# A 16-unit attention layer: six units' probabilities turned by 32x32 squares through DRAM, two table copies moved, bias windows kept as raw runs

## The reference

```python
def _na_mixer(h, hc, w_in, rpb, w_out, need_ctx_out):
    q, k, v, g = jnp.split(h @ w_in, 4, axis=-1)          # 16 heads of 64
    kc, vc = jnp.split(hc @ w_in[:, WIDTH:3 * WIDTH], 2, axis=-1)
    ...
    s_loc = s_loc + bias[None]                            # rpb by relative place, inside a window
    s_ctx = jnp.einsum('brqhd,bchd->bhrqc', q, kc)
    logits = jnp.concatenate([s_loc, s_ctx], axis=-1)
    p = jax.nn.softmax(logits, axis=-1)
    o = p_loc @ v + p_ctx @ vc                            # written here as products
    y = (o * jax.nn.silu(g)) @ w_out
```

## Time and profile before

| | us |
|---|---|
| median of 3 runs | 1814.83 (1814.77 to 1815.89) |
| the profiled execution, its own time | 1815.61 |
| its span in the profile | 1813.8 |
| PE busy in the span | 1793.3 |
| DVE, ACT, POOL busy | 954.2, 901.5, 1366.0 |
| the attention loop, first scores to the last turned unit | 303.9 to about 375.5 of the span |

### The profile page before, as it was taken

One profiled execution on the slowest core, in us unless ns is written; L12 is line 12 of the kernel. 1 busy time (PEld: TensorE's weight loads), 2 busy tenths in 40 slices (PEclk: granted clock), 3 DMA queues, 4 the chain that ended last, 5 costly groups with the idle time before them and its releaser, 6 DMA issues.

```text
span 1813.8 us, 24988 instructions
## 1 busy us (share of the span) xinstructions
PE 1793.3 (99%) x9274; PEld 1477.5 (81%) x9274; DVE 954.2 (53%) x1756; ACT 901.5 (50%) x1329; POOL 1366.0 (75%) x568
## 2 busy tenths in 40 slices
PE   6999999999999999999999999999999999999999
PEld 5888888887889888887788888888888878888887
DVE  4673766778755524866653230713095876143152
ACT  3324424674455644456554644464445565555452
POOL 2624544559968898977689798969897867888885
PEclk9999999999999999999999999999999999999999
DMA  9863885749775775565665566567655666656663
GB/s 366 291 210 94 270 310 163 198 141 312 244 277 200 211 221 191 180 198 168 209 186 192 179 195 191 193 187 234 191 193 185 192 190 182 196 160 210 190 195 128
DMA packets 206457, 372.91 MB, mean 206 GB/s; under 512 B 33508, under 2 KB 59092, under 8 KB 205780
## 3 DMA queue, kind: packets, MB, share of 16 engines
q1 hardware_dynamic: 203328, 363.69, 63.5%
q10 hardware_dynamic: 3028, 7.86, 1.2%
HBM read 367.27 MB, written 9.28 MB: 208 GB/s over the span
## 4 chain that ended last, share of the span: by engine, by line
PE 97%; DVE 2%; DMA 0%; issue 0%; ACTq 0%; ACT 0%; POOL 0%; DVEq 0%
PE ps L1300 26%; PE ps L1302 25%; PE ps L1301 25%; PE ps L1426 3%; PE ps L1427 3%; PE ps L1428 3%; PE ps L1992 1%; PE ps L1993 1%; PE ps L1994 1%; PE ps L1348 1%; PE ps L1697 1%; PE ps L1918 1%; PE ps L1668 1%; PE ps L1678 1%; PE ps L1962 1%; PE ps L1558 1%
## 5 line engine op out<-in xcount | busy, mean ns | idle before, releaser
L659 POOL TENSOR_TENSOR w_lo<-raw,w_hi 128x1024 fp32r<-128x1024 f32 x556 | 1347.1, 2461 | 397.4 <-ACT w_hi L697 376.2
L1300 PE MATMUL ps<-w_hi,act_rows_r 128*128 128x512 f32 x2064 | 814.8, 395 | 3.2 <-POOL w_lo L659 3.1
L1302 PE MATMUL ps<-w_hi,act_rows_r 128*128 128x512 f32 x2064 | 805.2, 390 | 0.0
L1301 PE MATMUL ps<-w_lo,act_rows_r 128*128 128x512 f32 x2064 | 804.6, 390 | 0.0
L697 ACT ACTIVATE w_hi<-raw 128x1024 fp32r<-128x1024 f32 x556 | 571.1, 1058 | 371.0 <-DMA raw<-in_ffn_w_up 100.8
L1300 PEld LDWEIGHTS ps<-w_hi,act_rows_r 128*128 128x128 f32 x2064 | 388.2, 188 | 90.4 <-issue 9.1
L1302 PEld LDWEIGHTS ps<-w_hi,act_rows_r 128*128 128x128 f32 x2064 | 388.0, 188 | 82.0
L1301 PEld LDWEIGHTS ps<-w_lo,act_rows_r 128*128 128x128 f32 x2064 | 388.4, 188 | 77.7
L2647 DVE STREAM_TRANSPOSE ps<-proj 32x256 f32<-32x256 f32 (+1 forms) x384 | 166.5, 434 | 6.5
L2628 DVE TENSOR_TENSOR proj<-proj,ps 128x1024 f32<-128x1024 f32 (+1 forms) x18 | 20.4, 1132 | 252.2 <-PE ps L1302 247.9
L1426 PE MATMUL ps<-act_rows_r,w_hi 128*128 128x512 f32 (+1 forms) x288 | 101.3, 352 | 0.0
(11 more groups left out here) (245 smaller groups left out, 1554.0 us busy)
## 6 DMA issues: line engine op xcount, KB each, us to landing
raw<-in_w_in SPq DMA_DIRECT2D x120, 512.0 KB, 3.9
raw<-in_ffn_w_gate SPq DMA_DIRECT2D x88, 512.0 KB, 4.4
raw<-in_ffn_w_up SPq DMA_DIRECT2D x88, 512.0 KB, 4.4
raw<-in_ffn_w_down SPq DMA_DIRECT2D x88, 512.0 KB, 4.2
proj<-in_ada_w SPq DMA_DIRECT2D x39, 512.0 KB, 7.9
pt<-in_ada_w SPq DMA_DIRECT2D x38, 512.0 KB, 6.4
raw<-in_pool_w_in SPq DMA_DIRECT2D x32, 512.0 KB, 7.3
raw<-in_na_w_in SPq DMA_DIRECT2D x32, 512.0 KB, 4.9
```

The source lines that it names most:

```text
L659: pool.tensor_tensor(w_lo[:, s, :], raw[:, s, :], w_hi[:, s, :].bitcast(F32), ALU.subtract).then_inc(lo_done, 1)
L1300: pe.matmul(o, h, hi, start=start, stop=False)
L1301: pe.matmul(o, h, lo, start=False, stop=False)
L1302: return pe.matmul(o, c, hi, start=False, stop=stop)
```

## The change

Units 0, 2, 4, 6, 8 and 10 (`NA_SQUARED`) no longer pass through `na_turned` and `pt`. In place of it DVE turns the unit's 128x1024 probabilities in 32x32 squares inside their partitions (into `bias[:, 2048:3072]`), ACT issues a save of these 512 KB to the DRAM tensor `na_squares` in turn u+3 (`keep_squares`), and in turn u+4 four transfers of 32 partitions each that place the squares where they belong (`place_squares`, into `proj`); the values of the unit are made in turn u+5, two turns later than before, from four runs of 32 values. One DRAM tensor and one SBUF place serve all six units, so each step waits for the step before it: the save for the squares of its unit and for the placing of the unit before, the placing for the save and for the values of the unit before, DVE's next squares for the last save. `na_c(i)` after a squared unit i-3 waits for DVE's turning, where it waited for PE's.

`load_bias` loads, for each head and row parity, one raw run of 219 values per partition into `proj` (4 transfers in place of 8), and `masked` reads 4 overlapping windows out of that run and writes the masked bias in two instructions. The loads wait for `masked(hp-2)`, and `masked(hp)` now waits for `na_l(2hp-3)`; the first two pairs' loads move from group 7 to group 12 of the layer's input projection. `keep_rel(l)` moves from the attention loop to the first FFN of transformer layer l, behind its first 8 weight loads; `tables_of` waits for it one weight pair later.

```diff
+NA_SQUARED = (0, 2, 4, 6, 8, 10)
...
+    na_squares = nc.dram_tensor("na_squares", (P, 1024), F32, kind="Internal").ap()
...
         def na_out_bank(u):
-            return 2 if u < NA_UNITS - 3 else 4
+            return 3 if u == NA_SQUARED[-1] else 2 if u < NA_UNITS - 3 else 4
+        def na_due(i):
+            return [u for u in range(NA_UNITS - 1) if u + (5 if u in NA_SQUARED else 3) == i]
+        def na_last_of(k):
+            return 4 * k + 2 if 4 * k + 2 in NA_SQUARED else 4 * k + 3
+        def na_placed_rows(dims, at=0, rows=slice(0, P)):
+            return free(proj[rows, 0:1], dims, CTX_RES + 2 * D + at)
+        def bias_windows(hp, dims, at=0, rows=slice(0, P)):
+            return free(proj[rows, 0:1], dims, CTX_RES + D + (hp % 2) * 512 + at)
...
             def load_bias(hp):
-                for h, t, rq in ((h, t, rq) for h in range(2) for t in range(NT) for rq in range(2)):
...
+                if hp >= 2:
+                    sp.wait_ge(bias_masked, hp - 1)
+                for h in range(2):
+                    for rq in range(2):
+                        src = bass.AP(na_rows.tensor, (2 * hp + h) * RPB_HEAD + (5 - rq) * RPB_C + 15, [[NA_ROW - 1, GRID_W], [1, RPB_SPAN]])
+                        sp.dma_start(bias_windows(hp, [[1, RPB_SPAN]], h * 256, slice(64 * rq, 64 * rq + 64)), src).then_inc(bias_in[hp % 2], 16)
...
-                    if l == 0:
-                        sp.wait_ge(rel_in, 16 * 2 * LAYERS)
+                    sp.wait_ge(rel_in, 32 * (l + 1))
...
-                    sp.wait_ge(dve_done, dve_s.count(("na_l", 2 * j + 1)))
                     load_bias(j + 2)
                 send(I["na_w_out"][0][j * P:(j + 1) * P, :], [[1, D]])
-                if j in (1, 3):
-                    keep_rel(j // 2)
+            sp.wait_ge(na_kept, 16 * len(NA_SQUARED))
...
+                        if tables and pair == 0:
+                            keep_rel(l)
                         if tables and pair < 3:
                             tables_of(l, pair)
...
             def masked(hp):
...
+                if hp >= 2:
+                    pool.wait_ge(dve_done, dve_s.count(("na_l", 2 * hp - 3)))
+                for t in range(NT):
+                    last = pool.tensor_tensor(free(bias[:, 0:1], [[512, 2], [GRID_W, 4], [1, GRID_W]], (hp % 2) * 1024 + t * SEQ),
+                                              bias_windows(hp, [[256, 2], [RPB_C, 4], [1, GRID_W]], 2 * RPB_C * (1 - t)),
+                                              free(na_mask[:, 0:1], [[0, 2], [GRID_W, 4], [1, GRID_W]]), ALU.add)
+                last.then_inc(bias_masked, 1)
...
+                def keep_squares(u):
+                    act.wait_ge(dve_done, dve_s.count(("na_sq", u)))
+                    if u:
+                        act.wait_ge(na_placed, 64 * (u // 2))
+                    act.dma_start(na_squares[:], bias[:, 2048:3072]).then_inc(na_kept, 16)
+                def place_squares(u):
+                    act.wait_ge(na_kept, 16 * (u // 2 + 1))
+                    if u:
+                        act.wait_ge(pe_done, pe_s.count(("na_out", u - 2)))
+                    for kq in range(4):
+                        act.dma_start(na_placed_rows([[256, 4], [1, 256]], 0, slice(32 * kq, 32 * kq + 32)),
+                                      bass.AP(na_squares.tensor, 256 * kq, [[1024, 32], [32 * 1024, 4], [1, 256]])).then_inc(na_placed, 16)
...
-                        if i >= 3:
+                        if i - 3 in NA_SQUARED:
+                            act.wait_ge(dve_done, dve_s.count(("na_sq", i - 3)))
+                        elif i >= 3:
                             act.wait_ge(pe_done, pe_s.count(("na_t", i - 3, 1)))
...
+                    if i - 3 in NA_SQUARED:
+                        keep_squares(i - 3)
+                    if i - 4 in NA_SQUARED:
+                        place_squares(i - 4)
...
             def na_values(u):
-                pe.wait_ge(dve_done, dve_s.count(("na_pt", u, 0)))
-                pe.wait_ge(act_done, act_s.count(("na_pt", u, 1)))
+                if u in NA_SQUARED:
+                    pe.wait_ge(na_placed, 64 * (u // 2 + 1))
+                else:
...
-                        last = pe.matmul(ps[c * HD:(c + 1) * HD, bank, 0:P], v, pt[:, o:o + P], start=k == 0, stop=k == 3)
+                        maps = na_placed_rows([[256, 4], [1, 32]], 32 * (4 * c + k)) if u in NA_SQUARED else pt[:, o:o + P]
+                        last = pe.matmul(ps[c * HD:(c + 1) * HD, bank, 0:P], v, maps, start=k == 0, stop=k == 3)
...
-                    if i >= 2:
+                    due = na_due(i)
+                    for u in due[:-1]:
+                        na_values(u)
+                    if i >= 2 and i - 2 not in NA_SQUARED:
                         na_turned(i - 2)
-                    if i >= 3:
-                        na_values(i - 3)
+                    for u in due[-1:]:
+                        na_values(u)
...
                 def turned(u):
...
+                    if u in NA_SQUARED:
+                        dve.wait_ge(act_done, act_s.count(("na_e", u, 1)))
+                        if u:
+                            dve.wait_ge(na_kept, 16 * (u // 2))
+                        dve.transpose(free(bias[:, 0:1], [[32, 8], [256, 4], [1, 32]], 2048),
+                                      na_rows_of(u, [[P, 8], [32, 4], [1, 32]])).then_inc(dve_done, dve_s.one(("na_sq", u)))
+                    else:
...
```

More of the change, by code:

```diff
@@ L23 @@
 RPB_HEAD = 15 * RPB_C
+RPB_SPAN = 5 * RPB_C + GRID_W
 LAYERS = 2
@@ L235, in program @@
         decay_in = sem("decay_in")
+        na_kept, na_placed = sem("na_kept"), sem("na_placed")
         maps_kept, maps_in = ([sem(f"{n}{k}") for k in range(2)] for n in ("maps_kept", "maps_in"))
@@ L508, in narrow @@
                                 x_made(sp, prev, 1, nb)
[L509 to L512, removed]
+                        if stage == "na_in" and g == 12:
+                            sp.wait_ge(scratch_in, 16)
+                            load_bias(0)
+                            load_bias(1)
                         if stage == "na_in" and g == 16:
@@ L662, in masked @@
             def masked(hp):
-                pool.wait_ge(bias_in[hp % 2], 128 * (hp // 2 + 1))
-                both = free(bias[:, 0:1], [[SEQ, 4], [1, SEQ]], (hp % 2) * 1024)
-                pool.tensor_tensor(both, both, free(na_mask[:, 0:1], [[0, 4], [1, SEQ]]), ALU.add).then_inc(bias_masked, 1)
+                pool.wait_ge(bias_in[hp % 2], 64 * (hp // 2 + 1))
+                if hp >= 2:
[5 more added lines that the diff above has]
+                last.then_inc(bias_masked, 1)
             pool.wait_ge(dve_done, dve_s.count(("first_gains", 0, 1)))
@@ L962, in na_layer @@
                         u = i - 2
[L963 to L967, removed]
+                        if u not in NA_SQUARED:
+                            act.wait_ge(pe_done, pe_s.count(("na_t", u, 1)))
+                            if u >= 2:
+                                act.wait_ge(pe_done, pe_s.count(("na_out", u - 2)))
+                            act.activation(pt[:, (u % 2) * 1024 + 512:(u % 2) * 1024 + 1024], ps[:, 7, :],
+                                           ACT.Copy).then_inc(act_done, act_s.one(("na_pt", u, 1)))
                         if i == NA_UNITS:
@@ L1682, in na_values @@
             def na_values(u):
-                pe.wait_ge(dve_done, dve_s.count(("na_pt", u, 0)))
-                pe.wait_ge(act_done, act_s.count(("na_pt", u, 1)))
+                if u in NA_SQUARED:
+                    pe.wait_ge(na_placed, 64 * (u // 2 + 1))
+                else:
+                    pe.wait_ge(dve_done, dve_s.count(("na_pt", u, 0)))
+                    pe.wait_ge(act_done, act_s.count(("na_pt", u, 1)))
                 bank = na_out_bank(u)
@@ L2438, in turned @@
                 def turned(u):
[L2439 to L2442, removed]
+                    if u in NA_SQUARED:
[5 more added lines that the diff above has]
+                    else:
+                        dve.wait_ge(pe_done, pe_s.count(("na_t", u, 0)))
+                        if u >= 2:
+                            dve.wait_ge(pe_done, pe_s.count(("na_out", u - 2)))
+                        dve.tensor_copy(pt[:, (u % 2) * 1024:(u % 2) * 1024 + 512], ps[:, 6, :]).then_inc(dve_done, dve_s.one(("na_pt", u, 0)))
                     dve.wait_ge(act_done, act_s.count(("na_e", u, 1)))
@@ L2476, in gated @@
                     dve.wait_ge(pe_done, pe_s.count(("tp", "nag", 0, k)))
-                    dve.wait_ge(dve_done, dve_s.count(("na_o", 4 * k + 3)))
+                    dve.wait_ge(dve_done, dve_s.count(("na_o", na_last_of(k))))
                     z = ps[:, NA_Z_BANK[k], :].rearrange("p (c n) -> p c n", c=2)
@@ L2490, in na_layer @@
                         dve.wait_ge(pe_done, pe_s.count(("na_s", i)))
-                        if i >= 3:
+                        if i >= 3 and i - 3 not in NA_SQUARED:
```

(7 more changed lines are left out.)

## The result

The changed kernel takes 1820.25 us, median of 7 runs (1819.06 to 1821.52); the kernel before took 1814.77 in its 7 runs beside them (1814.32 to 1815.89). The ratio is 1.0029, 95% interval 1.0018 to 1.0040: 5.5 us slower. The forecast was 1810.4 with a range to 1815.0; sign and size are nearly those of the slower rival (1820.8).

The account below looks back on a forecast made before the run. PE was taken to bound the kernel, busy 1793.3 of 1813.8 us. Removed turns -5.8, start +0.95 and late saves +0.4 gave -4.45 us, from 1814.83 to 1810.4; range 1808.9 to 1815.0.

Parts of the forecast that it names:

- the slower rival: Attention loop: saves fall in with weight loads; circle 9.8 us, 10.9 us lost, net +6.0, 1820.8; chance 0.13.
- the circle: Attention loop: save, three issues and last placing through one DRAM tensor take 7.0 us, fitting a turn pair of 7.85.
- late saves next to weight loads: Attention loop: saves delayed beside weight loads cost 0.4 us in all.
- The save of 3.2: Attention loop: a 512 KB save to DRAM takes 3.2 us, as the same size where less is in flight.
- the placing, taken as 2.5: Attention loop: the 128 KB placing takes 2.5 us, between 2.3 and the bias loads' 3.0.
- The removed turns: PE in the attention loop: six units lose eight turns each, 0.97 us per unit, gaining 5.8 us.
- The start: Turns 2 and 3: scores(3) and scores(4) wait for `na_l(2)` and `na_l(3)`, losing 0.5 and 0.45 us, 0.95 in all.
- The values from runs of 32: PE's value products in the attention loop: reading runs of 32 out of `proj` costs nothing, 273 ns either way.
- DVE's squares: DVE in the attention loop: squares at 1024 columns take 1.30 us in place of a 0.68 copy, and fit.
- the table copies: First FFN: 1280 KB copies taking 8.7 us are covered by eight weight slots; uncovered, up to 2 x 8.7 us.
- POOL and the bias loads: Attention loop: POOL's masking in two instructions and SP's 32 bias loads instead of 64 cost nothing.
- ACT's issues: ACT in the attention loop: five issues of 0.43 run beside other work, no cost; 2.7 us in all if they stop it.

Follow-up runs that it names:

- two in DRAM: Changed kernel with unit 0 keeping its turns, no wait of `pt` copies for unit 10's values, two DRAM tensors, one SBUF place: 1811.68 us, ratio 0.9981.
- both repairs: Changed kernel with two DRAM tensors and two SBUF places for squares, and no wait of `pt` copies for unit 10's values: 1812.88 us, ratio 0.9986.
- from unit 2: Changed kernel with two DRAM tensors, two SBUF places, no wait of `pt` copies for unit 10's values, unit 0 keeping its turns: 1811.72 us, ratio 0.9974.
- no squares: Changed kernel with `NA_SQUARED` empty; raw bias runs, later first bias loads and table copies in the FFN stay: 1815.06 us, ratio 1.0000.
- no old wait: Changed kernel in which unit 12's copies to `pt` no longer wait for the values of unit 10: 1816.44 us, ratio 1.0015.
- two places: Changed kernel with two DRAM tensors and two SBUF places for the squares, the wait of `pt` copies kept: 1814.34 us, ratio 1.0000.

## Why the prediction was wrong

**The step that failed is the circle.** It was put together as 3.2 + 1.3 + 2.5 = 7.0 us, bounds 6.2 and 8.4, "against 7.85", with "late saves next to weight loads I price at 0.4 us in all", for which no row stood. Measured in the changed kernel it is 5.17 + 1.58 + 3.26 = 10.0 us in one pair and 7.7 in the next. The save of 3.2, borrowed from a weight load of that size, is right for one condition: ahead of the load, in "two in DRAM", it is 2.9 to 3.3. The mistake was to give it one length. A circle with 0.85 us of slack, whose phase decides the length of its longest leg, has no such slack: the save that comes 2.2 us later against its load takes 1.3 us longer (4.44 against 3.1). And the placing, taken as 2.5, reached 4.4 with one tensor and 4.2 with two. The slower rival had the mechanism, but that its price of 6.0 stands beside a measured 5.5 is luck in good part. It was to decide from a circle of 8.8, which is the mean measured; there its own sum has 0.95 x 5 = 4.75 us of waits, which only cancel the gain, and 4.4 were measured. The rest of the 5.5 came from a wait that it did not have, from the two smaller terms below, and from the 1.7 us that the traces do not show. What spoke against that rival, "some eight weight loads in the loop, not one per save", has the right count and the wrong conclusion: SP sends one for each odd turn, and each save goes out in an odd turn. The row to look at was the issue times of those loads beside the turns, not their number.

**A wait was overlooked.** The prediction followed the new waits and who stands behind them, but not the old ones whose event the change moves: `pt` copies wait for `na_out(u-2)`, which went from turn u+1 to u+3. For units 2 to 10 no copies are made any more; unit 12 alone has them, after a squared unit 10. Removing that wait gave 3.8 us by the medians, 2.5 by the ratios. By the profile 0.95 is the wait and 1.6 the clock at its lower level behind it, 2.6 together, which the ratios bear out; what more the medians have stays open.

**The removed turns** were priced at 0.97 each. The timeline of PE in the run with two DRAM tensors shows an even turn with nothing else in its way:

```profile
340.67 0.39 PE L1717 MATMUL ps<-act_rows_r 64*128 64x256 f32 x2
...
342.85 0.39 PE L1351 MATMUL ps<-w_hi,act_rows_r 128*128 128x512 f32 x1
343.17 1.09 PE L1750 MATMUL ps<-pt,proj 128*64 128x128 f32 x16
344.19 0.39 PE L1717 MATMUL ps<-act_rows_r 64*128 64x256 f32 x2
```

It lasts 3.52 us; before, turn 10, the same one, had 348.54 - 344.15 = 4.39. The gain is 0.87 a unit, not 0.97: the values start 0.32 us behind the last gate product, where before, in turn 11, the turns started 350.96 - 350.73 = 0.23 behind it. Five units by 0.87 are 4.4, and the loop gained 4.3: the term was right within a tenth.

**The start** was priced at 0.95 lost of unit 0's 0.97. Turns 2 and 3 last 3.45 and 3.92 us, where 2.83 and 3.37 had been possible: 1.2 lost. Scores(4) do wait 0.48 us for `na_l(3)`; in turn 2 PE waits 0.19 us not ahead of scores(3) for `na_l(2)`, as forecast, but ahead of the late queries' turn for `proj_r`. Unit 0 is not a gain of nothing but a loss of 0.3; in "both repairs" 0.28 us of waiting for its placing comes on top, and the loop is 0.6 longer than in "from unit 2".

**What held.** The values from runs of 32 take 1.09 us for 16 records as from `pt`; DVE's squares 1.24 us (1.30 estimated); no wait of PE that is new stands behind 380 us, though the table copies took 10.3 us in the FFN, where 8.7 had been read the earlier trace rows; POOL and the bias loads cost nothing ("no squares"). ACT's issues, taken as lying beside its other work, did not: ACT stands behind them before its `split`, but PE did not wait on that.

## What to carry to other kernels

Where a buffer closes a loop (produce, save, place, use, save again), a second buffer in the loop is the first thing to price, and in DRAM it takes nothing from SBUF: here a second DRAM tensor, with its waits, was worth 5.3 us, from 2.1 lost to 3.2 won against the kernel before. A transfer's length is not one number when other transfers run in step with it; read its issue time against theirs in the same turn. And when a change moves an event, look for every old wait on that event, also those that no longer protect anything.

## What the runs showed of the hardware beyond that

**One transfer's length by its place beside another.** 512 KB from SBUF to DRAM took 2.6 to 2.9 us with SP's loads held back. Over all runs with squares it took 2.7 to 3.3 when issued 0.3 to 1.0 us ahead of the 512 KB load (but for two saves), 3.9 to 4.0 when 0.1 us ahead, 3.7 to 5.6 when 0.5 to 1.6 us behind it, and 3.3 to 4.2 when 2.2 to 2.9 us behind.

**Packets of the queue "instruction" fall in with the longest saves.** In five saves a packet of 16 KB of the queue that the profile calls "instruction" moved within the first 2.3 us, and these took 4.7 to 5.6 us: the 5.56 above, the last save of the changed kernel (5.02) and of "no old wait" (4.70), and the two exceptions, in "two places" (5.10, 0.34 us ahead of its load) and "from unit 2" (4.77, 0.35 ahead). With the same lead and no such packet "two in DRAM" has 3.3. So of the three saves of 5 us in the changed kernel the last may be slow by this and not by the load alone; of the first two (5.17 and 4.92) one has such a packet only in its last 0.4 us, the other none. That the packet is the cause was not tried.

**DVE beside several instructions of POOL.** In the profiled execution of "both repairs" DVE's work stretched out between the layers, in the timeline:

```profile
577.86 11.78 POOL L685 TENSOR_TENSOR w_lo<-raw,w_hi 128x1024 fp32r<-128x1024 f32 x5
...
582.87 7.32 DVE L3095 TENSOR_TENSOR proj<-x_res,act_rows 128x512 f32<-128x512 f32 x1
...
590.24 0.66 PE L1405 MATMUL ps<-ident,proj 128*128 128x128 f32 x4 [2.78 <-DVE proj L3095]
```

A multiplication of DVE with two operands in SBUF, 0.69 us in other places of this line, took 7.32 and ended 0.55 us after a row of POOL's remainders did (577.86 + 11.78 = 589.64). PE waited 3.3 us for it, and the granted clock was 0.50 from 592 to 594 us; outside the loop this execution is about 5 us longer than that of "from unit 2" (1815.3 - 67.9 against 1809.6 - 67.3). In the kernel before the same line has at most 2.68 us, in the eight other traces at most 2.70. The Trainium skill, page "SBUF — State Buffer", section "SBUF: two separate sides", says that such an instruction and one of GpSimd that reads SBUF share a pair of ports, and that whichever starts first has it for its whole instruction. By that DVE would wait for one of POOL's, 2.4 us; the 2.68 us of before agrees, the 7.32 is more than two of them and does not. That this is the cause of the upper heap of that run's times is argued from one trace and was not tried.
